# Attention outputs computed turned: values stationary on the array, row-sum division moved ahead of the transposition

## The reference, cut to what matters

```python
def _attend_block(q, k, v, scale):
    s = jnp.einsum('bqkrd,bskd->bkrqs', q, k).astype(jnp.float32) * scale
    p = jax.nn.softmax(s, axis=-1).astype(v.dtype)
    return jnp.einsum('bkrqs,bske->bqkre', p, v)
...
o_mla = attend(q_m, k_m, kv[..., MLA_NOPE:], ...)   # latent attention: 8 heads, q and k 96 wide, values 64
o_gqa = attend(gq, gk_all, gv_all, ...)             # grouped attention: 8 query heads on 2 key heads, all 64 wide
...
br = jnp.stack([o_mla, o_gqa, o_r, o_d], axis=2)    # with retention and differential attention
merged = jnp.sum(gates * jnp.einsum('btnw,nwd->btnd', br, lp['w_br']), axis=2)
```

## Time and profile before

| | |
|---|---|
| runs, median | 2130.18 us (2119.91 to 2142.24, 3 runs) |
| profiled execution | 2137.14 us, span 2135.6 us |
| mean granted TensorE clock | 0.949 |
| PE matmul busy | 1878.0 us (88%) |
| PE weight loads busy | 1322.2 us (62%), beside matmuls |
| DVE, ACT, POOL busy | 1138.8, 884.0, 397.6 us |

### The profile page before, as it was taken

How to read it: one execution, slowest core, us unless ns; L and a number is a source line. 1 busy time by engine, 2 the same in 40 slices (tenths; PEclk the granted TensorE clock), 3 DMA queues, 4 the chain that set the end, 5 groups by cost and what they waited for, 6 DMA issues and landing times.

```text
span 2135.6 us, 26671 instructions
## 1 busy us (share of the span) xinstructions
PE 1878.0 (88%) x8784; PEld 1322.2 (62%) x8784; DVE 1138.8 (53%) x1660; ACT 884.0 (41%) x1510; POOL 397.6 (19%) x381
## 2 busy tenths in 40 slices
PE   6998998999977999999179989889999779999990
PEld 3886666888764665555048866568887545555550
DVE  2345557454445666665533455665444646555655
ACT  3342346433342555554133423563333435555541
POOL 2004211400004122221220051214000031221212
PEclk9999998999989999999689999989999999999995
DMA  8443270643435999998374323607434459999984
GB/s 299 149 133 101 99 239 25 199 166 118 158 125 161 344 377 378 378 375 335 133 277 151 119 94 129 228 16 236 138 119 138 174 183 361 363 369 360 363 300 162
DMA packets 120461, 457.62 MB, mean 214 GB/s; under 512 B 13040, under 2 KB 20880, under 8 KB 88880
## 3 DMA queue, kind: packets, MB, share of 16 engines
q1 hardware_dynamic: 96672, 384.86, 50.3%
q0 software_dynamic: 20192, 65.15, 10.3%
q10 hardware_dynamic: 3504, 6.40, 0.8%
HBM read 411.69 MB, written 44.71 MB: 214 GB/s over the span
## 4 chain that ended last, share of the span: by engine, by line
PE 30%; DMA 8%; DVE 5%; issue 3%; ACT 3%; POOL 1%; SPq 0%; DVEq 0%; ACTq 0%; POOLq 0%
PE psum L1878 17%; DMA W<-in_w_exp_gu 7%; PE psum L1818 6%; PE psum L2123 3%; PE psum L1825 2%; PE psum L1843 1%; DMA W<-in_w_mod 1%; POOL slot_tokens L911 1%; ACT scratch_split L1250 1%; DVE W_split L1377 0%; DVE zf L1800 0%; DVE zf L1616 0%; DMA W<-in_w_in 0%; ACT hT L987 0%; DMA zf<-token_rows,vm 0%
## 5 line engine op out<-in xcount | busy, mean ns | idle before, releaser
L1377 DVE TENSOR_TENSOR W_split<-W,W_split 128x2048 fp32r<-128x2048 f32 (+3 forms) x96 | 224.8, 2344 | 407.4 <-ACT W_split L1018 407.4
L1878 PE MATMUL psum<-W_split,qT_split 128*128 128x512 f32 (+3 forms) x1536 | 404.4, 376 | 9.7 <-ACT hT L987 8.1
L1018 ACT ACTIVATE W_split<-W 128x2048 fp32r<-128x2048 f32 (+3 forms) x96 | 175.9, 1838 | 414.1 <-PE psum L1878 345.1
L1878 PEld LDWEIGHTS psum<-W_split,qT_split 128*128 128x128 f32 x1536 | 283.6, 189 | 59.8 <-ACT hT L987 8.7
L1818 PE MATMUL psum<-W,zf 128*96 128x512 f32 (+1 forms) x560 | 258.7, 605 | 30.2 <-ACT zf L1278 27.1
L1878 PE MATMUL psum<-W_split,scratch_split 128*128 128x512 f32 x864 | 275.7, 391 | 0.6 <-DVE hT_split L1372 0.6
L1768 DVE TENSOR_TENSOR W_split<-W,qT_split 128x2048 fp32r<-128x2048 f32 x64 | 146.7, 2292 | 231.0 <-ACT qT_split L1250 231.0
L1250 ACT ACTIVATE qT_split<-W 128x2048 fp32r<-128x2048 f32 x64 | 122.6, 1915 | 259.3 <-DMA W<-in_w_exp_gu 221.6
L1878 PE MATMUL psum<-W_split,hT_split 128*128 128x512 f32 x576 | 211.0, 394 | 5.8 <-DVE scratch_split L1575 5.8
L2123 PE MATMUL psum<-qT_split,hT_split 128*96 128x512 f32 x512 | 198.9, 450 | 6.3 <-issue 6.3
L2123 PE MATMUL psum<-W_split,hT_split 128*96 128x512 f32 x512 | 202.9, 396 | 0.0
(11 more groups left out here) (315 smaller groups left out, 2635.6 us busy)
## 6 DMA issues: line engine op xcount, KB each, us to landing
W<-in_w_exp_gu SPq DMA_DIRECT2D x128, 1024.0 KB, 11.0
W<-in_w_exp_down SPq DMA_DIRECT2D x64, 1024.0 KB, 9.6
W<-in_w_in SPq DMA_DIRECT2D x60, 1024.0 KB, 5.2
W<-in_w_mod SPq DMA_DIRECT2D x48, 1024.0 KB, 4.9
y_slots<-zf SPq DMA_DIRECT2D x64, 384.0 KB, 8.7
W<-in_w_br SPq DMA_DIRECT2D x16, 1024.0 KB, 5.1
y_slots<-kT POOLq DMA_DIRECT2D x2, 6144.0 KB, 33.4
W<-in_w_out SPq DMA_DIRECT2D x8, 1024.0 KB, 5.0
```

The lines of the kernel that those rows point to most:

```text
L1018: nc.scalar.activation(high(j), piece(SPLITS[j]), ACT.Copy).then_inc(S["high_ready"], 1)
L1377: V.tensor_tensor(piece(SPLITS[j], Wr), piece(SPLITS[j]), high(j).bitcast(F32), ALU.subtract).then_inc(S["low_ready"], 1)
L1878: ins = nc.tensor.matmul(bank(job, piece_size(key)[1]), act_part[:, k0 + k, t * P:(t + 1) * P], w_part[:, k, :], start=first and (k, i) == ...
```

## The change

The values become the stationary operand and the transposed exponentials move, so that `O` comes out with the head's 64 features on the partitions and the queries along the row. Two heads share a bank: the even one takes partitions 0 to 63, the odd one 64 to 127, each tile t its 128 columns. The bank is emptied once, by ACT, after the last map of the pair. The outputs stand in `z` as they are needed by the branch product, and branches 0 and 1 need no `oT` jobs. Because queries are no longer on the partitions of `O`, the division by the row sum is done on the exponentials in SBUF, by DVE, ahead of their transposition. The `O` jobs take banks 5 and 6 in turn; the ring for the other jobs of the maps has 5 banks.

```diff
+    def add_part(self, key, bank):
+
+        assert key not in self.number
+        self.number[key] = len(self.number)
+        self.banks[key] = bank
+        self.before[key] = self.last.get(bank)
...
+def ends_pair(mp):
+
+    return mp[1] % 2 == 1 and mp[2] == T - 1
...
+BANK_O = 5, 6
...
+TURNED_BRANCHES = 2
...
-                jobs.add(("O",) + m[i - 4], "dve")
+                key = ("O",) + m[i - 4]
+                if ends_pair(m[i - 4]):
+                    jobs.add(key, "act", BANK_O[m[i - 4][1] // 2 % 2])
+                else:
+                    jobs.add_part(key, BANK_O[m[i - 4][1] // 2 % 2])
...
-        if g == "mb":
-            jobs.turn_over(BANK_MOD)
+        jobs.turn_over(BANK_O[0])
         softmax_maps(g)
+        if g == "ma":
+            jobs.turn_over(8)
...
-        for k in range(4):
+        for k in range(4 if n >= TURNED_BRANCHES else 0):
...
+        def turned_out(n, k):
+
+            return z[:, :, OUT_COLS[n] + k * P:OUT_COLS[n] + (k + 1) * P]
...
-                                    act.wait_ge(*emptied(("O",) + m[i - 5]))
+                                    act.wait_ge(S["p_scaled"], SCALED_AT[m[i - 5]])
...
+                            if i >= 4 and ends_pair(m[i - 4]):
+                                empty_pair(m[i - 4])
...
+                    def empty_pair(mp):
+                        g, h, _ = mp
+                        key = ("O",) + mp
+                        act.wait_ge(*filled(key))
+                        if g == "mb":
+                            act.wait_ge(S["cache_out"], 16 * 6)
+                        dst = turned_out(1 if g == "g" else 0, h // 2 + (HALF // 2 if g == "mb" else 0))
+                        nc.scalar.activation(dst, bank(key, T * P).rearrange("p (t n) -> p t n", t=T), ACT.Copy).then_inc(S["act_emptied"], 1)
...
-                                act.wait_ge(*filled(("oT", n, k)))
-                                nc.scalar.activation(oT_split[0][:, k], bank(("oT", n, k), 384), ACT.Copy).then_inc(S["oT_high"], 1)
+                                if n < TURNED_BRANCHES:
+                                    act.wait_ge(*filled(("br", n - 1, 1, T - 1) if n else ("R", T - 1)))
+                                    src = turned_out(n, k)
+                                else:
+                                    act.wait_ge(*filled(("oT", n, k)))
+                                    src = bank(("oT", n, k), 384).rearrange("p (t n) -> p t n", t=T)
+                                nc.scalar.activation(oT_split[0][:, k].rearrange("p (t n) -> p t n", t=T), src, ACT.Copy).then_inc(S["oT_high"], 1)
...
+                    def scale_map(m, i):
+
+                        r, n = i % 5, P * len(keys_of(m[i][2]))
+                        p = Pb[:, (i % 3) * 384:(i % 3) * 384 + n]
+                        dve.wait_ge(*emptied(("S",) + m[i]))
+                        link(V.reciprocal(rrec[:, r:r + 1], rsum[:, r:r + 1]))
+                        V.tensor_scalar(p, p, rrec[:, r:r + 1], None, ALU.mult).then_inc(S["p_scaled"], 1)
...
-                            if i >= 4:
-                                key, s = m[i - 4], (i - 4) % 5
-                                dve.wait_ge(*emptied(("S",) + key))
-                                link(V.reciprocal(rrec[:, s:s + 1], rsum[:, s:s + 1]))
-                                dve.wait_ge(*filled(("O",) + key))
-                                V.tensor_scalar(out_cols(*key), bank(("O",) + key, HD), rrec[:, s:s + 1], None,
-                                                ALU.mult).then_inc(S["dve_emptied"], 1)
+                            if 1 <= i < len(m) + 1:
+                                scale_map(m, i - 1)
...
-                            dve.wait_ge(S["cache_out"], 16 * 6)
...
+                                src = turned_out(n, k) if n < TURNED_BRANCHES else bank(("oT", n, k), 384).rearrange("p (t n) -> p t n", t=T)
+                                high_part, low_part = (v[:, k].rearrange("p (t n) -> p t n", t=T) for v in oT_split)
+                                V.tensor_tensor(low_part, src, high_part.bitcast(F32), ALU.subtract
+                                                ).then_inc(S["oT_low" if n < TURNED_BRANCHES else "dve_emptied"], 1)
...
-                                weigh_values(m[i - 4], i % 2)
+                                weigh_turned(m[i - 4], i % 2)
                             if 2 <= i < len(m) + 2:
                                 j = i - 2
-                                pe.wait_ge(*emptied(("S",) + m[j]))
+                                pe.wait_ge(S["p_scaled"], SCALED_AT[m[j]])
...
+                    def weigh_turned(mp, s):
+
+                        key = ("O",) + mp
+                        g, h, t = mp
+                        bank_free(key)
+                        pe.wait_ge(*emptied(("PT",) + mp))
+                        multiply(psum[HD * (h % 2):HD * (h % 2) + HD, J.bank(key), t * P:(t + 1) * P],
+                                 [(values(g, h, kt), PTb[:, s * 384 + b * P:s * 384 + (b + 1) * P])
+                                  for b, kt in enumerate(keys_of(t))]).then_inc(S["psum_filled"], 1)
...
-                            pe.wait_ge(*emptied(("oT", n, 3)))
+                            if n < TURNED_BRANCHES:
+                                pe.wait_ge(S["oT_low"], 4 * n + 4)
+                            else:
+                                pe.wait_ge(*emptied(("oT", n, 3)))
```

More of the change, by code:

```diff
@@ L342 @@
             MAX_AT[_key] = len(MAX_AT) + 1
+SCALED_AT = {}
+for _g in ("ma", "mb", "g"):
+    for _m in MAPS[_g]:
+        SCALED_AT[_m] = len(SCALED_AT) + 1
 GATES = [(n, c, t) for n in range(NBR) for c in range(2) for t in range(T)]
@@ L418, in trunk @@
         names += ["dec_scaled", "mixture_rows", "post_root", "pre_root", "zeros_ready", "zeros_out", "halves_used", "high_ready", "low_ready", "h_split", "oT_high", "mgT_high",
-                  "gu_half_used", "gu_high", "gu_low", "x_high"]
+                  "oT_low", "p_scaled", "gu_half_used", "gu_high", "gu_low", "x_high"]
         landed_names = [f"piece_landed{i}" for i in range(RAW)] + [f"gu_landed{s}{h}" for s in range(2) for h in range(2)] + ["dn_landed0", "dn_landed1"]
@@ L1937, in weigh_values @@
                         pe.wait_ge(*emptied(("PT",) + mp))
-                        multiply(bank(key, F_DV if g == "d" else HD),
+                        multiply(bank(key, F_DV),
                                  [(PTb[:, s * 384 + b * P:s * 384 + (b + 1) * P], values(g, h, kt))
```

8 lines of the change are left out of this document (removed).

## The result

The changed kernel takes 2181.99 us (median of 4 runs, 2180.95 to 2183.44); the kernel before, measured beside it, 2127.8 us (4 runs, 2119.91 to 2142.24). The ratio is 1.0247, with a 95% interval from 1.0214 to 1.028: slower by 54 us. The forecast of 2164 us had the direction; the result lies at the very end of its range (2133 to 2182), 18 us above it. The profiled executions are 45.7 us apart (span 2181.3 against 2135.6).

What follows compares the result with a forecast made beforehand. PE was taken to bound the maps. Terms of 32.8 + 2.6 + 2.4 + 2.0 - 2.6 - 3.0 gave +34.2 us: 2171.3 us against the profiled execution, 2164 against the median; range 2133 to 2182.

Steps and rivals of the forecast that it cites:

- PE is the bound, and added PE time is paid in full.: In `ma`, `mb` and `g`: PE sets the pace, with only 3.2 us idle per layer, so added PE time shows fully.
- So each change of shape costs 0.19 to 0.20 us.: In the maps: PE entering or leaving the half-array shape for `O`, 84 changes per layer at 0.195 us, 32.8 us together.
- the wider products: `O` matmuls in the maps: 128 moving columns instead of 64, 0.08 us more per head, 2.6 us in all.
- The first PT of a group, 0.4 us.: At the start of each map group `PT` waits for reciprocal and scaling, 0.4 us each, 2.4 us in all.
- given back for banks: In `g`: half of PE's 2.84 idle us, taken as waits for a bank, saved: 1.5 us per layer, 3.0 together.
- POOL's lock, costed beside `ma` alone.: In `ma`: DVE's scalings wait 0.50 us on average for POOL instructions, mostly covered, 1 us per layer, 2 together.
- In branches 0 and 1 ACT and DVE read the outputs from SBUF [...] Both cost nothing.: Reading outputs in branches 0 and 1, under 16 us of gate products, and ACT's added copies in the maps: 0 us.
- Branch 1.: Its 12 transpositions go, saving 1.31 us per layer, 2.6 together; at branch 0 nothing is saved.
- a free shape: Rival, in the maps: half of the array is free to enter and leave; 32.8 us fall away, 2137 us; chance 0.23.
- the price: Rival, in the maps: each change of shape costs half as much, 2148 us; chance 0.10.
- the lock: Rival, in `ma`: POOL excluding DVE's scalings sets the pace, 13 us on top, 2177 us; chance 0.05.
- the clock: Rival, in `ma`: new bubbles bring 1.2 GHz throughout, 40 us more over both layers, 2204 us; chance 0.04.

Runs made afterwards that it cites:

- e11: Changed kernel with POOL's head norms after branch 0's low parts and POOL's decays after the tenth scaling of the grouped maps: 2155.4 us, ratio 1.0105.
- e2: Changed kernel with the stationary operand of `O` 128 columns wide, so the array keeps its full shape: 2167.1 us, ratio 1.0187.
- e1: Changed kernel with POOL's head norms of branches 2 and 3 started only after DVE has written branch 0's low parts: 2156.8 us, ratio 1.0116.
- e4: Changed kernel with the stationary operand of `O` 128 columns wide and POOL's head norms after branch 0's low parts: 2135.9 us, ratio 1.0012.
- e9: Kernel before, with DVE's reciprocal ahead of the transposition and `PT` waiting for it, `O` still divided leaving PSUM: 2139.8 us, ratio 1.0022.
- e3: Changed kernel with POOL's rotation of the differential q and k only after the last scaling of `ma`: 2185.5 us, ratio 1.0254.
- e7: Changed kernel with full-width `O` operand, head norms after branch 0's low parts, and POOL's rotations after the last scaling of `ma`: 2144.9 us, ratio 1.0039.
- e8: Kernel before with only the division moved ahead of the transposition, and POOL's rotations after the last scaling of `ma`: 2145.5 us, ratio 1.0063.
- e10: Changed kernel with full-width `O` operand, head norms after branch 0's low parts, and DVE scaling map i-1 ahead of map i's maximum: 2158.5 us, ratio 1.0127.
- e5: Kernel before with only the division moved: DVE scales exponentials ahead of their transposition and copies `O` out as it is: 2145.6 us, ratio 1.0052.

## Why the prediction was right in its direction and short in its size

That the result lies within the stated range, by 0.01 us, is luck. The shapes cost half of what was forecast, and terms that the forecast put at nothing or too low made up more than that.

- **PE is the bound, and added PE time is paid in full.** Right in `mb`. In `ma`, at the full clock, the half array takes 20.28 us (e11, second layer) and the full one 18.59 (e2, first layer): 1.7 us for 22 changes, where 22 x 0.14 would be 3.1, so part is covered there too; at the lower clock the two are 2.8 apart. In `g` more than half was covered: with POOL's decays out of the way `g` takes 48.88 us with the half array and 46.68 with the full one, 2.2 us for 38 changes, where `mb` pays 28.50 - 25.32 = 3.2 for 24. Three waits of PE for ACT's exponentials in `g`, 1.9 us in the first layer before, are not there afterwards; that they took up part of the new work fits this, and is not shown by a run of its own.
- **"So each change of shape costs 0.19 to 0.20 us."** The mechanism is right; the size was 0.14 us at the full clock (0.85 / 6), 0.13 in `mb` (3.2 / 24), 0.06 net in `g`. The way out was read rightly (0.19). The way in was not: the 0.53 us of the earlier trace rows run from start to start of weight loads, and were held against 0.33 between matmuls. PE's own rows at that place have 0.43, that is 0.10 for the way in, as for the new shape:

```profile
254.99 0.50 PE L1825 MATMUL psum<-const,Pb 128*128 128x128 f32 x3
255.42 1.06 PE L1843 MATMUL psum<-W,silT 128*32 128x512 f32 x8
```

  The shapes cost (2.8 + 3.2 + 2.2) x 2 = 16 us in place of 32.8, where `ma` goes from 24.43 (mean of the changed kernel and e1, which is the same up to there) to 21.65 (e4); this leaves out the wider products, 0.14 for each of 32 heads or at most 4.5 us, which e4 has too and for which the forecast had 2.6.
- **The Trainium skill (TensorEngine Tiling (Array Packing), Key Properties)** says that changing the tiling mode drains TensorE. The runs agree that the change of shape is what costs: with the same columns and one shape the 0.85 us per head are gone. That it is a drain no row shows, and the page names no price.
- **The first PT of a group, 0.4 us.** The scaling's wait is 0.74 us at the start of `g` and its work shows later too: `mb` and `g` together pay 1.16 + 1.12 = 2.3 us a layer in e4, where the forecast had 0.8 less 1.5 given back for banks. e4 still has 3.5 us more in each `ma`, part of it the clock; at the full clock it is 2.3 (18.59 in e2, 16.30 in e9). From before to e4 the maps cost 11.8 us; the forecast's 2.4 + 2.0 - 3.0 + 2.6 were 4.0. No run isolates the 3.0 us given back for banks; the waits that the view names in `g` before end with ACT's exponentials, not with a bank.
- **POOL's lock, costed beside `ma` alone.** In `ma` it is a wash (e3, e7, e8); a scaling there waits 0.23 us on average ((16.33 - 13.55) / 12), where the forecast had 0.50. It was overlooked at the start of `g`, where POOL's decays begin with the last `O` of `mb`: 2.9 us a layer, 5.7 in all.
- **"In branches 0 and 1 ACT and DVE read the outputs from SBUF [...] Both cost nothing."** This is the step that failed. The read was hidden only as long as it is short; beside POOL it took 13.64 us instead of 1.94, and e1 gives 25 us back. The prediction had the row that warns (two copies of 128x128 in 2.32 us, ending with POOL's instructions) and drew the consequence for the scaling only. The weights' split in the kernel before, 4.26 us beside POOL at this very place, was in the trace too. The Trainium skill (SBUF — State Buffer, Who interferes with whom) also says that a DVE instruction with two inputs in SBUF contends with a GpSimd instruction that reads SBUF; moving one operand of L1587 from PSUM to SBUF is just that case, and the trace agrees, at 3.4 us in place of 0.55. That page should have been applied to every operand that the change moves.
- **Branch 1.** 1.3 us a layer forecast; 1.2 measured in the first layer and in both of e1 and e4, 0.5 in the second. At branch 0 PE does not wait the forecast 1.9 us for `hT_split` but 1.17 and 0.69.
- **The sum.** 16 (shapes) + 12 (division and wider products) + 6 (decays) + 24 (branch 0) - 2 (branch 1) = 56 us. The forecast's rivals: a free shape is refuted; the price was nearer to three quarters at the full clock and to half over all; the lock and the clock each came true in part, the lock in other places than the rival put it. Of the 6.3 us by which `ma` is longer, some 2.3 are the clock by an estimate: at 1.00 the changed form took 20.28 us (e11) and the form before, with the wait of the division, 16.30 (e9), 4.0 apart. What sets the clock of `ma` stays open: with one kernel it took 16.30 and 23.40 us.

No version is faster than the kernel before. With both prices gone e4 ends level, and what the idea can save is 12 transpositions of branch 1, 2.5 us in all.

## What to carry to other kernels

When a change moves an operand from PSUM to SBUF, look up what POOL does at that time, for each instruction that reads it: here DVE instructions of 0.55 us with two SBUF operands lasted as long as POOL's 3 to 4 us, and held up all that stood behind them on DVE. Narrowing the stationary operand to half of the array isn't free where its neighbours use all of it: it cost 0.09 us in and 0.19 us out here, and if the banks allow, keep the full width and ignore half of the output. When prices are read from start to start, take both starts from the same kind of row. Behind PE's idle time, look for a slower clock as well.

## What the runs showed of the hardware that was not expected

- The lock between DVE and POOL takes whole instructions: four subtractions of 0.55 us took 3.11 to 3.86 us each beside POOL instructions of 2.79 to 3.70, and a scaling of 0.29 us took 1.54 beside POOL instructions of 1.47.
- A change of shape costs less on the way in than on the way out: 0.09 and 0.19 us for 128*64. What rows there are of the other shapes agree: 0.10 into 128*32, 0.19 out of 64*128.
- A wait of PE costs more than its length. Behind the 8.9 us at branch 0 the next product took 10.7 instead of 8.2 us; behind 1.99 us in `g` the next product ran at 1.62 instead of 0.92. At the start of `ma` the granted clock is 0.50 (1.2 GHz) for 12 us in the changed kernel:

```profile
214.00:226.00 12.00, 10.12 (x27) 5.68 (x27) 7.56 (x18) 4.36 (x14) 11.29 (x12) 0.50 0.00 0
```

In the first layer of e2 and e9 and the second of e11, `ma` had 1.00 throughout. Ahead of it PE turns keys and queries, with two waits; they were 2.9 and 1.7 to 1.9 us there. In e11's first layer they were 2.9 and 3.2, and in the changed kernel, as in most others, 1.3 and 4.1, with a lower clock in `ma`:

```profile
211.36 2.79 PE L1868 MATMUL psum<-const,scratch 128*96 128x128 f32 x12 [4.07 <-DVE scratch L650]
```

```profile
212.60 1.52 PE L1835 MATMUL psum<-const,scratch 128*96 128x128 f32 x12 [1.66 <-DVE scratch L629]
```

The first line is the changed kernel's, the second that of e9; the same 12 transpositions take 2.79 us behind the long wait and 1.52 behind the short one. That the length of the wait alone decides is not shown: e10's first layer had 2.9 and 1.6 and a mean of 0.87 over `ma`, in which PE also waited 5.2 us; and the run with the division alone had 4.05 us and was at 1.00 again when `ma` began. With one kernel and in one execution the two layers' `ma` were 2 to 7 us apart in this way (20.66 and 22.81 in e5, 16.30 and 23.40 in e9), which is as much as the change's own terms there.
